# Averages of the norms' squares: one plain fp32 product replaced by two fp32r products of a split sum

## The reference, cut to what matters

```
def rmsnorm(x, g):
    xf = x.astype(jnp.float32)
    y = xf * lax.rsqrt(jnp.mean(xf * xf, axis=-1, keepdims=True) + EPS)
    return (y * g.astype(jnp.float32)).astype(x.dtype)

for l in range(2):                                   # first block
    h = h + 0.5 * swiglu(rmsnorm(h, ffn1_norm[l]), ...)
    u = rmsnorm(h, mix_norm[l]); z = u @ w_in[l]     # three mixers, gates
    h = h + merged @ w_out[l]
    h = h + 0.5 * swiglu(rmsnorm(h, ffn2_norm[l]), ...)
x = rmsnorm(h, final_norm)
h = rms_norm(x, even_norm_g)                         # second block, layer 0 (attention and a state space)
...
h = rms_norm(x, odd_norm_g)                          # layer 1 (gated linear attention)
```

## Time and profile before

| | |
|---|---|
| median of three runs | 1451.78 us |
| span of the profiled execution | 1450.2 us |
| TensorE products (PE) busy | 1444.7 us, 12390 |
| VectorE (DVE) busy | 1050.9 us, 1434 |
| ScalarE (ACT) busy | 782.0 us, 1014 |
| GpSimd (POOL) busy | 92.0 us, 73 |
| DMA | 261.37 MB, mean 180 GB/s |

### The profile page before, as it was taken

How to read it: one execution, slowest core, us unless ns; L and a number is a source line. 1 busy time by engine, 2 the same in 40 slices (tenths; PEclk the granted TensorE clock), 3 DMA queues, 4 the chain that set the end, 5 groups by cost and what they waited for, 6 DMA issues and landing times.

```text
span 1450.2 us, 28453 instructions
## 1 busy us (share of the span) xinstructions
PE 1444.7 (100%) x12390; PEld 1396.0 (96%) x12390; DVE 1050.9 (72%) x1434; ACT 782.0 (54%) x1014; POOL 92.0 (6%) x73
## 2 busy tenths in 40 slices
PE   9999999999999999999999999999999999999999
PEld 9999998999999999999999899999999999989978
DVE  7766686897876655766558689888787799666844
ACT  6444555565554444544436566455645655775753
POOL 0000000210000000000000020000000037300000
PEclk9999999999999999999999999999999999999999
DMA  8655545444555655555554544466655454435541
GB/s 328 229 183 195 188 155 206 146 146 150 199 197 191 204 180 198 201 181 200 190 199 139 197 146 155 165 215 225 204 182 197 146 198 153 144 106 176 194 139 59
DMA packets 38844, 261.37 MB, mean 180 GB/s; under 512 B 4672, under 2 KB 5184, under 8 KB 9152
## 3 DMA queue, kind: packets, MB, share of 16 engines
q1 hardware_dynamic: 38576, 259.54, 52.5%
q10 hardware_dynamic: 144, 0.00, 0.0%
HBM read 258.48 MB, written 1.05 MB: 179 GB/s over the span
## 4 chain that ended last, share of the span: by engine, by line
PE 99%; DVE 1%; ACT 0%; issue 0%; POOL 0%; POOLq 0%
PE ps L257 31%; PE ps L259 30%; PE ps L258 30%; PE ps L1539 1%; PE ps L1554 1%; PE ps L1530 0%; PE ps L1512 0%; PE ps L2422 0%; DVE w_low L231 0%; PE ps L923 0%; PE ps L2856 0%; PE ps L2443 0%; PE ps L2871 0%; PE ps L2868 0%; PE ps L2455 0%; PE ps L2402 0%
## 5 line engine op out<-in xcount | busy, mean ns | idle before, releaser
L224 ACT ACTIVATE w_high<-w_raw 128x2048 fp32r<-128x2048 f32 (+1 forms) x243 | 457.3, 1883 | 481.9 <-PE ps L259 478.6
L231 DVE TENSOR_TENSOR w_low<-w_raw,w_high 128x2048 fp32r<-128x2048 f32 (+1 forms) x240 | 550.4, 2294 | 202.8 <-ACT w_high L224 202.4
L257 PE MATMUL ps<-x,w_high 128*128 128x256 f32 x2224 | 623.6, 280 | 0.5 <-DVE w_low L231 0.4
L259 PE MATMUL ps<-x,w_low 128*128 128x256 f32 x2224 | 617.1, 277 | 0.0
L258 PE MATMUL ps<-x,w_high 128*128 128x256 f32 x2224 | 617.1, 277 | 0.0
L257 PEld LDWEIGHTS ps<-x,w_high 128*128 128x128 f32 x2224 | 418.3, 188 | 6.4 <-issue 4.8
L259 PEld LDWEIGHTS ps<-x,w_low 128*128 128x128 f32 x2224 | 419.2, 188 | 0.0
L258 PEld LDWEIGHTS ps<-x,w_high 128*128 128x128 f32 x2224 | 418.3, 188 | 0.7 <-issue 0.5
L257 PE MATMUL ps<-ffn_hid,w_high 128*128 128x256 f32 x528 | 145.7, 276 | 0.0
L258 PE MATMUL ps<-ffn_hid,w_high 128*128 128x256 f32 x528 | 145.7, 276 | 0.0
L259 PE MATMUL ps<-ffn_hid,w_low 128*128 128x256 f32 x528 | 145.7, 276 | 0.0
(11 more groups left out here) (482 smaller groups left out, 2134.8 us busy)
## 6 DMA issues: line engine op xcount, KB each, us to landing
w_raw<-in_weights SPq DMA_DIRECT2D x229, 1024.0 KB, 4.9
w_raw<-in_weights SPq DMA_DIRECT2D x10, 768.0 KB, 4.2
setup_first<-in_first SPq DMA_DIRECT2D x8, 256.0 KB, 4.8
w_raw<-in_weights SPq DMA_DIRECT2D x4, 512.0 KB, 5.3
even_second_vectors<-in_second SPq DMA_DIRECT2D x1, 1836.0 KB, 7.7
w_raw<-in_weights SPq DMA_DIRECT2D x2, 640.0 KB, 3.9
resid<-in_x SPq DMA_DIRECT2D x1, 1024.0 KB, 10.1
out<-resid SPq DMA_DIRECT2D x3, 256.0 KB, 2.4
```

What stands on the lines that cost most here:

```text
L224: act.activation(self.slot(self.wh, n)[:, f], self.slot(self.raw, n)[:, f], ACT.Copy).then_inc(self.hi_made, 1)
L231: dve.tensor_tensor(self.slot(self.wl, n), self.slot(self.raw, n), self.slot(self.wh, n).bitcast(F32), ALU.subtract).then_inc(self.lo_made, 1)
L257: pe.matmul(out, ah, bh, start=start, stop=False, skip_group_check=True)
L259: return pe.matmul(out, al, bh, start=False, stop=stop, skip_group_check=True)
```

## The change

The sum of the squares is written to `scratch` tile 2 instead of tile 0. VectorE then rounds it to fp32r (`parts` 0) and subtracts to get the remainder (`parts` 1). The buffer `parts` has the same place as the first two tiles of `scratch` (or of `even_q` in the second set). TensorE multiplies both parts by `share`, an fp32r copy of the 1/1024 matrix, which GpSimd makes at the start; TensorE waits for it once, behind its warm-up products. The first norm keeps its fp32 products.

```diff
-    def add_up(self, dve, sq):
+    def add_up(self, dve, sq, parts):
         ...
         c.dve_link(dve.tensor_tensor(sq[:, 0:2, :], sq[:, 0:2, :], sq[:, 4:6, :], ALU.add))
-        return dve.tensor_tensor(sq[:, 0, :], sq[:, 0, :], sq[:, 1, :], ALU.add)
+        c.dve_link(dve.tensor_tensor(sq[:, 2, :], sq[:, 0, :], sq[:, 1, :], ALU.add))
+        c.dve_link(dve.tensor_scalar(parts[:, 0, :], sq[:, 2, :], 1.0, None, ALU.mult))
+        return dve.tensor_tensor(parts[:, 1, :], sq[:, 2, :], parts[:, 0, :].bitcast(F32), ALU.subtract)
...
-    def average(self, pe, bank, sq):
-        return pe.matmul(self.c.bank(bank, SEQ), self.c.ones[:, 0, :], sq[:, 0, :], start=True, stop=True)
+    def average(self, pe, bank, parts):
+        return exact2(pe, self.c.bank(bank, SEQ), self.c.share[:, :], parts[:, 0, :], parts[:, 1, :])
...
+def exact2(pe, out, a, bh, bl):
+    pe.matmul(out, a, bh, start=True, stop=False, skip_group_check=True)
+    return pe.matmul(out, a, bl, start=False, stop=True, skip_group_check=True)
...
         pool.memset(c.eps[:, :], EPS).then_inc(self.ones_made, 1)
+        pool.wait_ge(self.ones_made, 1)
+        pool.tensor_scalar(c.share[:, :], c.ones[:, 0, :], 1.0, None, ALU.mult).then_inc(self.share_made, 1)
...
         for _ in range(WARM):
             pe.matmul(c.bank(B_DOWN, P), c.ones[:, 0, :], c.ones[:, 1, :], start=True, stop=True)
+        pe.wait_ge(self.share_made, 1)
...
-        self.ones = sb("ones", [P, 5, P])
+        self.ones, self.share = sb("ones", [P, 5, P]), sb("share", [P, P], F32R)
...
-    nc = bacc.Bacc("TRN2", target_bir_lowering=False, num_devices=1)
+    nc = bacc.Bacc("TRN2", target_bir_lowering=False, num_devices=1, dynamic_dma_scratch_size=8192)
```

More of the change, by code:

```diff
@@ L140, in __init__ @@
         self.xh, self.xl = self.x[:, 0], self.x[:, 1]
+        with ExitStack() as inner:
+            self.parts = inner.enter_context(nc.sbuf_tensor("sum_parts", [P, 2, SEQ], F32R))
         self.sq = sb("scratch", [P, DT, SEQ])
@@ L374, in add_up @@
         c.dve_link(dve.tensor_tensor(sq[:, 0:2, :], sq[:, 0:2, :], sq[:, 4:6, :], ALU.add))
-        return dve.tensor_tensor(sq[:, 0, :], sq[:, 0, :], sq[:, 1, :], ALU.add)
+        c.dve_link(dve.tensor_tensor(sq[:, 2, :], sq[:, 0, :], sq[:, 1, :], ALU.add))
+        c.dve_link(dve.tensor_scalar(parts[:, 0, :], sq[:, 2, :], 1.0, None, ALU.mult))
+        return dve.tensor_tensor(parts[:, 1, :], sq[:, 2, :], parts[:, 0, :].bitcast(F32), ALU.subtract)
     def add(self, dve):
         dve.wait_ge(*self.squared(4))
-        self.add_up(dve, self.c.sq).then_inc(self.c.sum_made, 1)
-    def average(self, pe, bank, sq):
-        return pe.matmul(self.c.bank(bank, SEQ), self.c.ones[:, 0, :], sq[:, 0, :], start=True, stop=True)
+        self.add_up(dve, self.c.sq, self.c.parts).then_inc(self.c.sum_made, 1)
+    def average(self, pe, bank, parts):
+        return exact2(pe, self.c.bank(bank, SEQ), self.c.share[:, :], parts[:, 0, :], parts[:, 1, :])
     def mean(self, pe):
         pe.wait_ge(*self.summed(1))
-        self.average(pe, self.bank, self.c.sq).then_inc(self.c.mean_made, 1)
+        self.average(pe, self.bank, self.c.parts).then_inc(self.c.mean_made, 1)
     def root(self, act):
@@ L423, in add, with average @@
         dve.tensor_tensor(sq[:, 4:6, :], sq[:, 4:6, :], sq[:, 6:8, :], ALU.add).then_inc(self.c.sum_made, 1)
-    def average(self, pe, bank, sq):
+    def average(self, pe, bank, parts):
         for k in self.LEFT:
-            mm = pe.matmul(self.c.bank(bank, SEQ), self.c.ones[:, 0, :], sq[:, k, :], start=(k == 0), stop=(k == self.LEFT[-1]))
+            mm = pe.matmul(self.c.bank(bank, SEQ), self.c.ones[:, 0, :], self.c.sq[:, k, :], start=(k == 0), stop=(k == self.LEFT[-1]))
         return mm
@@ L447, in add_more @@
         dve.wait_ge(self.e.sq_made, 1)
-        self.add_up(dve, self.e.sq).then_inc(self.e.sum_made, 1)
+        self.add_up(dve, self.e.sq, self.e.parts).then_inc(self.e.sum_made, 1)
     def mean(self, pe):
         pe.wait_ge(self.e.sum_made, 1)
-        self.average(pe, B_SUM + 1, self.e.sq).then_inc(self.c.mean_made, 1)
+        self.average(pe, B_SUM + 1, self.e.parts).then_inc(self.c.mean_made, 1)
         pe.wait_ge(*self.summed(1))
-        self.average(pe, B_SUM, self.c.sq).then_inc(self.e.first_mean, 1)
+        self.average(pe, B_SUM, self.c.parts).then_inc(self.e.first_mean, 1)
     def root(self, act):
@@ L843, in __init__ @@
         self.piece_in = [c.sem(f"piece_in{b}") for b in range(PIECES)]
-        self.half_in, self.tables_in, self.angle_made, self.sines_made, self.ones_made = (
-            c.sem(s) for s in ("half_in", "tables_in", "angle_made", "sines_made", "ones_made"))
+        self.half_in, self.tables_in, self.angle_made, self.sines_made, self.ones_made, self.share_made = (
+            c.sem(s) for s in ("half_in", "tables_in", "angle_made", "sines_made", "ones_made", "share_made"))
     def arrived(self, b):
@@ L1875, in __init__ @@
         self.cos = sb("cos", [P, S5_TILES, HALF])
+        with ExitStack() as inner:
+            self.parts = inner.enter_context(new("sum_parts", [P, 2, SEQ], F32R))
         with ExitStack() as inner:
```

## The result

The kernel after took 1453.72 us (median of 20 runs) against 1451.72 us before (20 runs): ratio 1.0013, 95% interval 1.0007 to 1.0019. One of the 20 runs took 1673 us with a granted clock of 0.81 from end to end, and one of the four of a later kernel, no_entry, took 2932 us; both are left out of the ratios and of what follows. So the change costs 2.0 us where I had said 0.4. The direction was right, and the time lies in the range of 1450.4 to 1454.2, but above the forecast's own spread of 1451.2 to 1453.0.

The account below looks back on a forecast made before the run. TensorE's queue was taken to set the end, other work counting only where TensorE waits: span 1450.24 - 1.10 + 1.56 = 1450.70 us, plus 1.54 to the median, 1452.24, stated as 1452.2; range 1450.4 to 1454.2.

Parts of the forecast that it names:

- TensorE's gain: Faster averages save 1.10 us: 0.20 per feed-forward norm, 0.15 per mixer, 0.20 in the odd layer, nothing at the FinalNorm.
- The length of the sum: On VectorE, the added rounding, subtraction and links make each `add_up` 0.78 us longer.
- The covers that were worked out at the five plain norms: Slack on VectorE hides the 0.78 us: 2.90 us in the feed-forward case, a 0.96 us reciprocal wait in the mixer.
- The FinalNorm: Two longer sums without cover there make `w_low`, and TensorE behind it, 1.56 us later.
- The odd layer: At its norm, 1.6 us of slack covers the longer sum's 0.78, and TensorE's average saves 0.20 us.
- A new wait in the odd layer: Sign of being wrong: a new TensorE wait showing in the odd layer (or in a mixer).
- The clock: Rival: TensorE's stalls at the FinalNorm bring a half-speed stretch costing 2.3 us, time 1454.5; chance 0.04.
- cut by the averages: Argument against a clock fall: the FinalNorm's two TensorE stalls, about 0.7 and 1.7 us, are separated by the averages.
- the rival that it holds on: Behind the averages the stream stays at 0.113 us a product, 0.5 us more saved, time 1451.7; chance 0.17.
- that it is lost for good: Feed-forward parts stay at 0.118 us a product, 6.5 us per norm, up to 19.5; chance 0.08.
- Start and placement: GpSimd's making of `share` at the start and the moved buffers cost nothing.

Follow-up runs that it names:

- no_entry: both_undone with the `ENTRY` offset of slot 2 in the feed-forward parts replaced by THREE; 1468.44 us, ratio 1.0113 to the kernel before.
- both_undone: Full change, but FinalNorm and the odd layer's norm back to plain fp32 averages and short sums; 1450.11 and 1451.23 us, ratios 0.9993 and 0.9995 to the kernel before.
- dve_only: Full change's longer VectorE sums, but TensorE averages the unsplit sum with one plain fp32 product; 1453.85 us, ratio 1.0016 to the kernel before.
- final_undone: Full change, but the FinalNorm back to plain fp32 averages and short sums; 1451.00 us, ratio 0.9996 to the kernel before.
- pe_only: Full change's two fp32r products, but VectorE makes no remainder and the rounded sum is used twice; 1450.32 us, ratio 0.9993 to the kernel before.
- filled: Full change plus 6 and 12 unused TensorE products in the two waits of the FinalNorm; 1453.43 us, ratio 1.0009 to the kernel before.

## Why the prediction was right or wrong

- **TensorE's gain**: right at the feed-forward norms. 0.43 became 0.23 us, and the three gave 0.19 to 0.20 each. The two mixers gave 0.17 and 0.39 where 0.15 each was said: the second holds 0.19 of a faster pace that was not foreseen there, so 0.17 for 0.15 in the first, where a part was given back, is partly luck. The 0.06 us that the sum takes for a signal stands in no row; the chain has 0.04 between `w_low` and TensorE at the FinalNorm and 0.14 in the odd layer. both_undone's 0.9 to 1.3 fits the 0.90 for these five, but cannot tell it from nothing.
- **The length of the sum**: right, 0.78 us, step by step. The covers that were worked out at the five plain norms held: in the first mixer the reciprocal's wait of 0.96 us shrank to 0.18, as said.
- **The FinalNorm**: right. 1.57 us against 1.56, by both waits foreseen: 0.62 us where about 0.6 was said, and 1.46 where "nearly 2" was. dve_only shows the 1.56 without TensorE's part (1.58).
- **The odd layer**: wrong, and the larger part of the miss. The step read "In the odd layer the sum is done at 1342.91 and wanted at about 1344.5: 1.6 against 0.78." That is true (TensorE found the sum ready in the kernel after too) and not enough: for the feed-forward norm I had gone on to the `split_low` queued behind the sum and to the slot that wants it, for the odd layer I had not. The `w_low` was wanted the moment it was ready. The rule of the prediction's own first paragraph, that work counts only where TensorE waits, led past it, since the list of waits had nothing at this place; the chain's row of 0.63, of which I kept only the first line, had "1345.15 0.11 issue" right behind it. Cost +0.76 instead of -0.20; dve_only's trace (0.78) and final_undone's chain show it, and the 0.9 between the medians of final_undone and both_undone fits. TensorE's saving of 0.20 does not exist there either (pe_only). A new wait in the odd layer was one of the prediction's own signs of being wrong, and it showed.
- **The clock**: named as a rival at 0.04 and priced at 2.3 us. It came in 8 of 19 runs and in 6 of 11 later ones, at 1.1 to 1.4 us. The price was high by about 1 us against the medians, 0.7 against the profile; the chance was far too small, since two stalls with four products between them were held to be "cut by the averages". filled shows the cause. That the time stayed in the range owes something to luck: with the fall in every execution the median would be at its edge, near 1454.1.
- **The pace**: in the feed-forward parts the rival that it holds on fell, and that it is lost for good fell too; in the mixers it did get faster. Its price was sound (17.6 us for all three where no slot catches it, 19.5 said), and what decides is the offset of the matrix, which the prediction gave as the reason against the first.
- **Start and placement**: right as far as the runs tell; pe_only has both and loses nothing.

The sum with the clock up reads 0.4 as predicted, + 0.96 for the odd layer, 1.36 us; the 11 runs with the clock at 1.000 are 1.3 us over the kernel before. With 8/19 of about 1.3 for the clock it is 1.9 us; the means of the runs differ by 1.9, the medians by 2.0.

## What to carry to other kernels

An edit that makes one engine shorter and another longer has to be followed in each place where it stands, and behind the longer step to everything queued there: what is late is the next thing on that engine, here a weight split that has nothing to do with norms. A chain that shows "issue" ahead of an instruction, 0.11 us here, may mark a place without slack, even where the list of waits is silent: look when its operands were ready. Where the bound engine's gain lies ahead of a wait, it is worth nothing, so the change should be kept only where the stream is dense: five norms of seven here, about 1 us under the kernel before by point estimate, though each interval alone still takes in 1.

## What the runs showed of the hardware

- A pause in which TensorE started 4 products in 2.7 us was followed, in 14 of 30 runs of the full change, by a stretch at half clock, seen in two profiles (3.4 us at 0.50 in each). With 22 products in the same time it never was (11 runs), with one wait of 1.27 us neither (11 runs).
- Three-product streams of the same shape run at 0.113 or at 0.118 us a product and stay in either for tens of microseconds; held in the slower one, three feed-forward parts cost 17 us. Two products with `share` where the change put it are enough to change the state; with the matrix 64 bytes further they are not.
- An average of 256 columns costs 0.43 us as one plain fp32 product and 0.23 us as two fp32r products; the rounding and subtraction of 128x256 on VectorE cost 0.78 us with their links (0.31, 0.43 and twice 0.02).
